# Two operand buffers moved by 480 and 640 bytes within SBUF

## What is computed

```
xn2 = rms_norm(h, ln2_g)
s   = scores of xn2 @ w_query against 2 x 128 sub-keys, per head
expert, gate = top 16 of the products, softmax          # 8 heads x 16 experts a token
a   = xn2 . u_tab[expert];  w = gate * gelu(a)
h   = h + sum(w * v_tab[expert])                        # 16384 experts
```

## The kernel before, in words

| buffer | before | after |
|---|---|---|
| wh, wl | 32 | 32 |
| xh | 480 | 0 |
| xl | 480 | 352 |
| row0_hi, row0_lo, mix and hidden parts | 64 | 64 |

## Time and profile before

### The profile page before, as it was taken

How to read it: one execution, slowest core, us unless ns; L and a number is a source line. 1 busy time by engine, 2 the same in 40 slices (tenths; PEclk the granted TensorE clock), 3 DMA queues, 4 the chain that set the end, 5 groups by cost and what they waited for, 6 DMA issues and landing times.

```text
span 1678.8 us, 32062 instructions
## 1 busy us (share of the span) xinstructions
PE 1605.4 (96%) x12800; PEld 1466.3 (87%) x12800; DVE 884.0 (53%) x1817; ACT 925.6 (55%) x1553; POOL 1195.5 (71%) x500
## 2 busy tenths in 40 slices
PE   8988999999999999999999999898999998999997
PEld 7876999999999998888888888677999986789997
DVE  6988445994366667777511116876220068752101
ACT  6666655445444445555566556665653447656533
POOL 5552777998877777777888887125888861268885
PEclk9999999999999999999999999999999999999999
DMA  7441655666655555555666664513666644146663
GB/s 260 131 129 39 197 167 177 190 194 194 183 174 176 175 176 174 176 175 171 195 194 188 191 194 142 179 53 121 190 197 188 187 155 165 52 140 195 192 189 113
DMA packets 79891, 280.42 MB, mean 167 GB/s; under 512 B 8704, under 2 KB 9472, under 8 KB 79488
## 3 DMA queue, kind: packets, MB, share of 16 engines
q1 hardware_dynamic: 79744, 278.38, 53.0%
HBM read 277.30 MB, written 1.05 MB: 166 GB/s over the span
## 4 chain that ended last, share of the span: by engine, by line
PE 83%; DVE 6%; issue 4%; ACT 3%; POOL 3%; DMA 0%; POOLq 0%; DVEq 0%; SPq 0%; ACTq 0%
PE ps L2660 14%; PE ps L2028 13%; PE ps L2329 10%; PE ps L2638 7%; PE ps L2667 7%; PE ps L2639 7%; PE ps L2643 7%; PE ps L537 6%; POOL wl L199 2%; ACT wh L184 1%; PE ps L2624 1%; PE ps L2626 1%; PE ps L371 1%; PE ps L2152 1%; PE ps L2122 1%
## 5 line engine op out<-in xcount | busy, mean ns | idle before, releaser
L199 POOL TENSOR_TENSOR wl<-slots,wh 128x1024 fp32r<-128x1024 f32 x236 | 572.4, 2429 | 342.0 <-ACT wh L184 333.9
L2438 POOL TENSOR_TENSOR wl<-slots,wh 128x1024 fp32r<-128x1024 f32 x256 | 618.3, 2418 | 126.1 <-ACT wh L2376 123.9
L2376 ACT ACTIVATE wh<-slots 128x1024 fp32r<-128x1024 f32 x256 | 271.8, 1062 | 351.3 <-issue 229.0
L184 ACT ACTIVATE wh<-slots 128x1024 fp32r<-128x1024 f32 x236 | 249.9, 1061 | 245.2 <-PE ps L2329 103.8
L2638 PE MATMUL ps<-xh,wh 128*128 128x256 f32 x1024 | 242.0, 279 | 0.0
L2639 PE MATMUL ps<-xl,wh 128*128 128x256 f32 x1024 | 238.8, 276 | 0.0
L2638 PEld LDWEIGHTS ps<-xh,wh 128*128 128x128 f32 x1024 | 192.3, 188 | 0.1
L2639 PEld LDWEIGHTS ps<-xl,wh 128*128 128x128 f32 x1024 | 192.3, 188 | 0.0
L2660 PE MATMUL ps<-wh,xh 128*128 128x512 f32 x508 | 160.1, 396 | 0.0
L2660 PE MATMUL ps<-wh,xl 128*128 128x512 f32 x508 | 158.0, 392 | 0.0
L2537 DVE TENSOR_TENSOR small<-ps,small 128x512 f16<-128x512 f32 x128 | 87.8, 686 | 108.2 <-PE ps L2626 108.2
(11 more groups left out here) (386 smaller groups left out, 3045.1 us busy)
## 6 DMA issues: line engine op xcount, KB each, us to landing
slots<-w SPq DMA_DIRECT2D x260, 512.0 KB, 3.5
slots<-wu SPq DMA_DIRECT2D x128, 512.0 KB, 3.6
slots<-wv SPq DMA_DIRECT2D x128, 512.0 KB, 3.5
arena<-bias SPq DMA_DIRECT2D x1, 2048.0 KB, 8.0
h<-xT SPq DMA_DIRECT2D x4, 256.0 KB, 5.8
arena<-keys SPq DMA_DIRECT2D x1, 1024.0 KB, 8.1
yT<-y_out SPq DMA_DIRECT2D x2, 512.0 KB, 2.7
layer<-consts SPq DMA_DIRECT2D x1, 800.0 KB, 5.2
```

The lines of the kernel that those rows point to most:

```text
L184: act.activation(self.hi[:, n % 2, :], self.slots[:, u % SLOTS, :], ACT.Copy).then_inc(self.rounded, 1)
L199: pool.tensor_tensor(self.lo[:, n % 2, :], self.slots[:, self.order[n] % SLOTS, :], self.hi[:, n % 2, :].bitcast(F32), ALU.subtract).then_ ...
L2376: act.activation(whv[:, r % 2, :], slots_v[:, r % SLOTS, :], ACT.Copy).then_inc(w_hi, 1)
L2438: pool.tensor_tensor(wlv[:, r % 2, :], slots_v[:, r % SLOTS, :], whv[:, r % 2, :].bitcast(F32), ALU.subtract).then_inc(w_lo, 1)
```

## The change

`xh` is placed 480 bytes lower and `xl` 640 bytes lower: an unused buffer of 120 columns is placed above `xh` and one of 40 columns above `xl`. Nothing else differs. `xh` then begins at 220672 and `xl` at 212320, which is above arena's end.

```diff
-        xh, xl = (ctx.enter_context(nc.sbuf_tensor(n, [P, DC * T], F32R, side="right")) for n in ("xh", "xl"))
+        def far(name, cols, dt=F32):
+            return ctx.enter_context(nc.sbuf_tensor(name, [P, cols], dt, side="right"))
+
+        far("above_xh", 120)
+        xh = far("xh", DC * T, F32R)
+        far("above_xl", 40)
+        xl = far("xl", DC * T, F32R)
```

## The result

The kernel became slower: 1709.26 us, median of four runs (1708.68 to 1711.84), beside 1681.83 us for the kernel before on the same chips. The ratio is 1.0157, 95% interval 1.0144 to 1.0170.

A forecast was written before the change was run, and what follows sets the result against it. TensorE's matmul pace was taken as the bound; xh's terms of 6.9, 4.2, 1.5 and 5.1 us, with xl at nothing, summed to +17.7 us on the profiled 1680.56, so 1698 us, range 1662 to 1710.

The forecast's parts named there:

- What bounds the kernel, and what is idle: Whole kernel: TensorE's matmul pace bounds it (96% busy); GpSimd has 0.3 us a row of slack in the expert stage.
- a sign of another engine: Expert stage: a change in GpSimd's 2.42 us or in the idle time would point to another engine.
- That the distance counts: TensorE's streams: pace depends on the moving operand's address minus that of the weights being loaded, modulo 512.
- Edit one, xl ... cost nothing, by the rule: Matmuls on xl: new distances 320 and 192 are multiples of 64, so moving xl 640 bytes costs 0.
- The rule, distance modulo 64: TensorE's operands: distances that are multiples of 64 have short paces, those 32 off have long ones; from four distances.
- A second term at nothing: line 2329: Layers' feed-forward run: uses neither xh nor xl, so its 84.02 us for 720 matmuls stays to the digit.
- The size for xh: Matmuls on xh: up rows +6.9 us, line 2028 +4.2, first block +1.5, down rows +5.1; together +17.7.
- The first block: Line 537, 368 matmuls on xh, a share of 0.6 counted as paying: +1.5 us.
- Rival 3, both buffers pay: All matmuls on xh and xl slow to 117.9 ns, down rows too: +33 us, 1714; chance 0.10 in full.
- Rival 1, far apart is cheap: Matmuls on xl at 320 and 192 run free of near collisions: kernel faster, around 1672 us; chance 0.32.
- Rival 2: Loop order or place, not distance, makes line 2329 and row 0 slow: nothing happens, 1683 us; chance 0.15.

The follow-up runs named there:

- e4: Against the kernel before: xh and xl at 0 modulo 512, wh, wl and all behind them 32 bytes higher, all distances kept; 1689.37 us, ratio 1.0043.
- e1: Against the kernel before: only xh to distance 480 from the weights, xl 512 bytes lower and still at 448; 1709.35 us, ratio 1.0162.
- e3: Against the kernel before: xh and xl both 128 bytes lower, at distance 320 from the weights; 1710.51 us, ratio 1.0169.
- e2: Against the kernel before: only xl 128 bytes lower, to distance 320 from the weights, xh stays at 448; 1706.23 us, ratio 1.0148.
- e12: Against the kernel before: 48 unused columns above xh, so xh and xl at distance 256 from the weights; 1713.24 us, ratio 1.0172.
- e5: Against the kernel before: arena 416 bytes higher, hidden parts from distance 32 to 448, xh and xl unmoved; 1678.14 us, ratio 0.9955.
- e6: Against the kernel before: 96 unused columns above xh, so xh and xl at distance 64 from the weights; 1706.93 us, ratio 1.0131.

## Why the prediction was right, and where it was not

**What bounds the kernel, and what is idle: right.** TensorE's busy time carried nearly all of it (31.1 of 31.3 us). GpSimd's unit kept its 2418 ns, and VectorE's and ScalarE's busy times moved by less than 1 us. GpSimd's idle time did grow, which the prediction had named as a sign of another engine; here it is GpSimd that waits longer.

**That the distance counts: right, and shown** by e4 against e1 and the change (1.0043 against 1.0162 and 1.0157, with xh at 0 modulo 512 in all three). The Trainium skill, page "SBUF — State Buffer", section "Who interferes with whom", says that PE never waits on anyone, and its table calls TensorE's two read ports, for the moving operand and for the weight load, independent. By that rule this change would cost nothing, and the measurement says otherwise: the pace depends on how TensorE's own two operands lie to each other.

**The step that failed: "Edit one, xl ... cost nothing, by the rule".** The rule, distance modulo 64, was drawn from four distances and is wrong. 320 itself has 117.8 in the up rows (e3), and 384, 256 and 0 are multiples of 64 and run at 118.7 to 120. By the rule e3 would have cost nothing, and it cost 28.9 us. The four distances fit a period of 256 just as well, and there 320 is 64. That alone would still have called it free, since line 570 ran at 113.3 with 64. What the prediction lacked is that one distance can have two paces, and that 64 and 320 rarely hold the short one. Measured from start to start over all up rows, xl's matmuls followed by a load of wh went from 113.7 to 117.7 ns: 1024 x 4.0 = 4.1 us where I had none. In the layers it was 704 x 4.0 = 2.8 us more, and in the down rows 508 x 3.2 = 1.6. With some 1 us in the first block that is 9 to 10 us for which the sum had nothing.

**A second term at nothing: line 2329.** It was to stay "to the digit". After the change it went from 84.02 to 84.81 us, and from 81.22 to 81.99 in the second layer, 1.6 us in all. The prediction says that this "would mean that the distance is not what counts". The runs say less: the distance counts (e4), and something besides it does too (e3's 120.0 at unchanged addresses).

**The size for xh: about right.** Forecast 6.9 us in the up rows; from 113.4 to 116.3 on 1024 and from 113.5 to 118.3 on 1024, some 8 us. In line 2028 4.2 forecast, 6.0 measured (1408 by 4.3). In the down rows 5.1 forecast; the matmuls followed by a load of xh rose by 1.8 ns (line 2660) and 4.3 ns (line 2667), 3.1 us: 32 is not as bad for 512 columns as row 0's 480 was. The first block, forecast at 1.5 us, took 5.6 more; less than 4 of it is the pace of line 543, and for the rest the two single executions give no cause.

**How the number came to fit.** The sum was added to the profiled execution (1680.56 us) and the forecast stated for the median (1682.96), on which 17.7 us would have given 1700.7. Against the profiled executions 31.3 us were measured, 13.6 more than the sum: xl's 9 to 10, line 2329's 1.6, some 3 more in the first block, and misses both ways in the xh terms (they are read from intervals with short waits in them and add up only roughly). That the time still fell inside the range, by 0.7 us, is luck rather than merit, and the sign came from a rule that was half wrong.

**Rival 3, both buffers pay, is what happened**, for the reason that I gave it half: e1 and e2 show that one buffer's place slows the other's matmuls. Its price, 117.9 ns for every matmul, was +33; the median gave 27.4, the profiled execution 31.3. I had it at 0.10 "in full", since I took the 117.9 ns groups of line 2028 for an accident. They were the clue: two paces at equal distances, so 113.3 was a state and could be lost.

**Rival 1, far apart is cheap, is refuted** by e12 in the up rows, and e2 and e3 show that 320 is no gain. The down rows are 2.2 ns better than before at 256, but equally so at 0, the nearest place, so this is no matter of being far. **Rival 2**, nothing happens, is refuted by the result, but its remark holds: something besides the distance does choose between 113.3 and 117.8, and in line 2329 between 116.7, 117.8 and 120.0.

**What stays open.** What picks the state after an interruption was not found: e4 and the kernel before differ in the long run of both layers with all distances equal, and e3 in line 2329 with all its addresses equal. Nor is it shown why the distance counts (that the two reads collide is a guess), or why 256 and 512 columns have opposite best places. Row buffers of their own at distance 0 for the down rows, beside xh and xl at 448, were not tried; 1524 matmuls by 2.2 ns would be 3.4 us, by my estimate. The mean of all down-row intervals, breaks between groups included, fell only by some 1.5 ns.

## What to carry to other kernels

Where TensorE is the bound, compare the pace (chain length over count) of loops with equal instructions: if they differ, look at the distance between streamed and loaded operands before looking at waits, and sweep it in steps of 16 or 32 bytes on the chip, for each width of matmul by itself. Do not draw a period from the places that the kernel happens to use. A kernel that nobody placed by design can stand in the best spot of all that were tried: each of the eleven other placings of xh and xl against the weights cost 1.3 to 1.7%, and even a shift that kept all distances cost 0.4% (e4). The pad that helped (e5) brought the remaining operands to the same distance.

## What the runs showed of the hardware that I had not expected

- fp32r matmuls of 256 columns with a weight load of 128 columns each settle into exact paces, held over hundreds of matmuls: 113.3, 116.7, 117.8 and 120.0 ns most often, 118.7 to 119.7 at distances 384, 416, 432 and 464. None of these streams reached the 106.7 ns that the prediction works out for 256 columns at 2.4 GHz.
- At one distance two or three of them can occur (113.3 and 117.8 at 448, 320 and 64; 116.7, 117.8 and 120.0 at 32, line 2329). Share of the matmuls on xh and xl in the short one: 83% before, 58% in e4, 68% in e5, 14% in e6, 3% in e3, 1% in e2, none at 0, 256, 384, 416, 432, 464 or 480 / 448.
- Two distances 256 bytes apart can be the same place: 0 and 256 agree in the up rows, the long run and the down rows (120.0, 120.4 and 226.7 ns).
- 16 bytes are enough to lose the short state (113.3 to 119.2 and 119.3 ns).
- With 512 columns the order is another: 226.7 at 0 and 256, 228.9 at 64, 230.0 at 80, 231.9 at 48, 233.3 at 96, 128, 192 and 448.
